# Identity products ahead of three of TensorE's waits in the attention and linear-attention units of a two-layer decoder step

## The reference

```
layer 0:  h = rmsnorm(x);  p = h @ w_in_even      (q, k, v of 4 heads; q, k, v, decay, gate of 4 linear heads)
          attention, prompt:  o = (softmax(q1 k1' + bias) - lam * softmax(q2 k2' + bias)) @ v      causal
          attention, sample:  the same against 4096 cached rows of k and v per sequence, by a page table
          a_out = rmsnorm(o, g_da)
          linear attention (chunks of 16):  att = tril(qe ke');  o = att v + qe S
                                            S = exp(b_last) * S + kd' v
          o = rmsnorm(o, g_gla) * silu(gate)
          x += rmsnorm([a_out, o] @ w_out_even);  x += rmsnorm(relu(h @ w_up)^2 @ w_down)
layer 1:  a gated recurrence with a width-4 convolution in place of attention, then the same kind of MLP
```

## Time and profile before

| | us |
|---|---|
| median of three runs | 1482.88 |
| the profiled execution's own time | 1480.3 |
| its span, first to last instruction | 1478.5 |
| TensorE busy, of the span | 1355.1 |
| VectorE busy | 1112.2 |
| ScalarE busy | 679.3 |
| Pool busy | 334.6 |

### The profile page before, as it was taken

One profiled execution on the slowest core, in us unless ns is written; L12 is line 12 of the kernel. 1 busy time (PEld: TensorE's weight loads), 2 busy tenths in 40 slices (PEclk: granted clock), 3 DMA queues, 4 the chain that ended last, 5 costly groups with the idle time before them and its releaser, 6 DMA issues.

```text
span 1478.5 us, 26838 instructions
## 1 busy us (share of the span) xinstructions
PE 1355.1 (92%) x10976; PEld 1216.4 (82%) x10976; DVE 1112.2 (75%) x1737; ACT 679.3 (46%) x1225; POOL 334.6 (23%) x268
## 2 busy tenths in 40 slices
PE   5999967878778898999999999899989999999997
PEld 5999933345333598999999999899988999999996
DVE  5799887775886626885968779789557868869695
ACT  4322245533343434544535446478444544445355
POOL 2567677775776200000000000000000000000000
PEclk9999978897776899999999999999999999999999
DMA  8788689999888831142231413222212132412321
GB/s 293 274 298 275 235 330 378 365 382 352 311 328 305 315 115 43 54 135 87 79 122 58 143 58 115 86 86 88 87 58 85 60 122 80 136 65 89 117 81 59
DMA packets 126865, 249.38 MB, mean 169 GB/s; under 512 B 5251, under 2 KB 107415, under 8 KB 110096
## 3 DMA queue, kind: packets, MB, share of 16 engines
q0 software_dynamic: 18432, 134.23, 24.0%
q1 hardware_dynamic: 105180, 109.46, 22.8%
q10 hardware_dynamic: 3132, 3.98, 0.9%
HBM read 239.99 MB, written 7.73 MB: 168 GB/s over the span
## 4 chain that ended last, share of the span: by engine, by line
PE 53%; issue 26%; DVE 9%; POOL 4%; ACT 4%; DMA 3%; POOLq 0%; ACTq 0%; SPq 0%; DVEq 0%
PE PS L2105 32%; PE PS L2183 10%; POOL PROD L764 3%; PE PS L2330 2%; DVE SC L1488 2%; DMA KV<-in_cache_v,CIDX 2%; PE PS L2491 1%; POOL KV L836 1%; PE PS L2414 1%; DVE ST L1726 1%; DMA XIN<-in_x_prompt 1%; ACT W_hi L894 1%; DVE W_lo L1421 1%; PE PS L2229 1%; PE PS L2317 1%
## 5 line engine op out<-in xcount | busy, mean ns | idle before, releaser
L2105 PE MATMUL PS<-H_hi,W_hi 128*128 128x260 f32 x1936 | 402.8, 288 | 20.8 <-DVE H_lo L1463 9.7
L2105 PE MATMUL PS<-H_hi,W_lo 128*128 128x260 f32 x1936 | 397.4, 286 | 0.0
L2105 PE MATMUL PS<-H_lo,W_hi 128*128 128x260 f32 x1936 | 396.9, 286 | 0.0
L2105 PEld LDWEIGHTS PS<-H_hi,W_hi 128*128 128x128 f32 x1936 | 305.5, 192 | 26.3 <-issue 22.6
L2105 PEld LDWEIGHTS PS<-H_hi,W_lo 128*128 128x128 f32 x1936 | 304.6, 192 | 0.0
L2105 PEld LDWEIGHTS PS<-H_lo,W_hi 128*128 128x128 f32 x1936 | 304.0, 191 | 0.0
L2183 PE MATMUL PS<-U_hi,G_hi 128*128 128x260 f32 x896 | 255.0, 285 | 0.3 <-DVE U_lo L1854 0.3
L2183 PE MATMUL PS<-U_hi,G_lo 128*128 128x260 f32 x896 | 253.5, 283 | 0.0
L2183 PE MATMUL PS<-U_lo,G_hi 128*128 128x260 f32 x896 | 252.1, 281 | 0.0
L1421 DVE TENSOR_TENSOR W_lo<-RAW,W_hi 128x2048 fp32r<-128x2048 f32 x58 | 132.9, 2291 | 99.9 <-ACT W_hi L894 99.8
L764 POOL TENSOR_TENSOR PROD<-KV,QB 128x1024 f32<-128x1024 f32 x64 | 153.9, 2405 | 98.6 <-DVE SC L1488 91.2
(11 more groups left out here) (329 smaller groups left out, 1939.9 us busy)
## 6 DMA issues: line engine op xcount, KB each, us to landing
RAW<-in_w_up SPq DMA_DIRECT2D x32, 1024.0 KB, 5.4
RAW<-in_w_down SPq DMA_DIRECT2D x32, 1024.0 KB, 4.9
RAW<-in_w_in_even SPq DMA_DIRECT2D x13, 1024.0 KB, 6.6
RAW<-in_w_in_odd SPq DMA_DIRECT2D x8, 1024.0 KB, 5.3
RAW<-in_w_out_even SPq DMA_DIRECT2D x4, 1024.0 KB, 8.5
RAW<-in_w_out_odd SPq DMA_DIRECT2D x4, 1024.0 KB, 4.8
x_saved<-X ACTq DMA_DIRECT2D x1, 2080.0 KB, 13.5
X<-x_saved SPq DMA_DIRECT2D x1, 2080.0 KB, 8.9
```

Source lines behind the costliest of these rows:

```text
L2105: t = MM_(PS[:, 2 * bank + j, 0:HALF], w[:, ch.wslot, k, cols], x[:, k, halves[j]], start=k == 0 and n == 0, stop=k == KT - 1 and n == 2)
```

## The change

A helper `keep_clock(count)` is added, and called at three places. It issues `count` products of the identity with itself into bank 3 of the PSUM, columns 0 to 127. Nobody reads these results: the next writer of the place starts its sum afresh. The products wait for nothing and signal nothing.

```diff
+        def keep_clock(count):
+
+            for _ in range(count):
+                MM_(PS[:, 3, 0:P], IDENT, IDENT, start=True, stop=True)
...
             if u >= 2:
                 normalise(u - 2)
                 pe.wait_ge(nev_done, u - 1)
+            keep_clock(3)
             pe.wait_ge(at_copied, u + 1)
...
         for u, (tb, hp) in enumerate(GLA_UNITS):
             if u:
+                keep_clock(4)
                 inner_products(u)
...
             pe.wait_ge(st_ready, 8 * u + 8)
             if u:
                 normalise(15 + u)
+            keep_clock(4)
             if u:
                 pe.wait_ge(nev_done, outputs_done(16 + u))
```

## The result

The change made the kernel slower. Eight runs of each gave a median of 1488.22 us (1482.86 to 1495.51) against 1481.61 us (1478.13 to 1484.05), a ratio of 1.0058 with a 95% interval of 1.0039 to 1.0077. The forecast was 4 us faster. Two things show at once: the sign is the other one, and the times of the changed kernel spread over 13 us where those of before spread over 6.

The account below looks back on a forecast made before the run. TensorE mostly bounds the kernel, with loads, VectorE and Pool also binding in the attention and linear units. Adding 17.0 us and getting 21.1 back nets -4.1: median 1482.9 becomes 1478.8 us, 8-in-10 range 1466 to 1492.

Parts of the forecast that it names:

- What a product costs: On TensorE, one further identity product in a group takes 0.22 us at the full clock, 0.425 at the low one.
- The cost on the path: Products delay the attention units by 7.4 us and the linear units by 9.6, together 17.0 us.
- the 60%: Attention units: share of the 48 products' 12.3 us taken as on the path, giving 7.4 us.
- cover: Linear units: 7 us of the products' 16.6 us hidden inside existing TensorE waits.
- What the clock gives back: Less low clock returns 6.2 us in the attention units, 11.9 in the linear units, 3.0 more: 21.1 us.
- the weaker term: Three long low-clock stretches, not counted as avoided, each end sooner: some 4.6 us in all, 3 taken.
- At twice the clock half of a busy time goes: In seven low-clock stretches of both unit stages, half of TensorE's 41.9 us busy time was the basis for the gain.
- My own first rival: No change that shows: VectorE and Pool set the pace in both stages, median at 1484 us; chance 0.29.
- The rule that everything behind 507 us merely shifts: From 507 us on the change touches nothing; the stretch from the output projection on stays at 971 us.
- The slower one: Clock falls behind waits for loads and Pool, attention products stay uncovered: +12 us, median 1495; chance 0.27.
- The break-even: 17 us must come back, meaning some 40 of the 118 us at the low clock must go.
- the first of my own signs: Prediction is wrong if the linear units' clock rises and their stage keeps its length, forecast at 147 to 151 us.

Follow-up runs that it names:

- e9: The changed kernel with each identity product reading one column instead of 128: 1.0079 of the kernel before.
- e5: The kernel before, unchanged, run and traced again: 1.0000 of the kernel before.
- e6: The changed kernel, run again without further edits: 1.0029 of the kernel before.
- e18: The changed kernel, run again beside e17: 1.0015 of the kernel before.
- e2: The changed kernel with only the linear units' 60 products, those of the attention units taken out: 0.9981 of the kernel before.
- e12: The changed kernel with six products instead of three in the attention units, four kept in the linear ones: 1.0054 of the kernel before.
- e16: Against the changed kernel, 48 attention products moved inside the copy wait, 32 linear ones kept in theirs, none ahead of the transposes: 1.0008 of before.
- e17: The changed kernel with the attention products moved inside the wait for the normalised output's copy, all 60 linear products kept: 0.9987 of the kernel before.
- e1: The changed kernel with only the attention units' 48 products, both calls of the linear units taken out: 1.0014 of the kernel before.
- e13: The changed kernel with 18 further products in the waits between the linear units and the output projection: 1.0059 of the kernel before.
- e15: The changed kernel, unedited, a further trace of one execution: 1482.89 us.
- e14: The changed kernel, unedited, a further trace of one execution: 1495.97 us.

## Why the prediction was wrong

The stages of the traces, in us. "None" are traces without products in that stage; for the last two rows it is the kernel before alone.

| | none | one column (e9) | changed kernel, 5 traces | attention products in the wait |
|---|---|---|---|---|
| attention units | 136.4, 137.9, 138.8, 135.1, 141.8: mean 138.0 | 143.8 | 138.0, 139.6, 143.2, 139.2, 138.7: mean 139.7 | 131.8, 133.2, 139.2, 132.2, 132.2: mean 133.7 |
| linear units | 115.7, 119.7, 117.4, 117.9: mean 117.7 | 122.5 | 112.0, 116.0, 122.6, 112.9, 116.1: mean 115.9 | |
| between them | 16.6, 16.3 | 17.2 | 17.9, 17.5, 17.8, 17.4, 18.2: mean 17.8 | |
| from the output projection on | 971.1, 970.8 | 971.3 | 973.4, 972.3, 970.4, 972.7, 974.7: mean 972.7 | |

**What a product costs** was right. In the kernel after a group of three took 0.94 us at the full clock and a group of four 1.16 us, so a further one costs 0.22, as forecast.

**The cost on the path** was put at 7.4 us for the attention units and 9.6 for the linear ones. With e9 as the kernel that pays and gets nothing, it is 143.8 - 138.0 = 5.8 us and 122.5 - 117.7 = 4.8 us, with 0.8 us between the stages: 11.4 us of 17.0. By its ratio e9 pays 0.79%, 11.7 us. This is one trace, and it holds more low clock than the kernel before, so it is an estimate. By it the 60% for the attention units was good, and the linear units had more cover than I counted.

**What the clock gives back** is the step that failed, by the size of its term. The prediction had 21.1 us. The fall of the low clock itself was forecast well: from the first product with v to the output projection it was 116 us before (133 in e5) and 78, 72, 102, 68 and 66 us in the five traces after, where I had 68, or less with the weaker term. But the time that came back is 143.8 - 139.7 = 4.1 us in the attention units (forecast 6.2) and 122.5 - 115.9 = 6.6 us in the linear ones (forecast 14.9 with the weaker term), 10.7 in all. "At twice the clock half of a busy time goes" holds for TensorE; that it "all lies on the path" doesn't. In the linear units low clock fell by some 38 us from e9 to the mean of the changed kernel, and TensorE's busy time by 15 us, from 108 to 93. Only 6.6 us of these reached the stage. The rest became idle time of TensorE, 14 us in e9 and 21 to 26 in the five traces, in waits for loads, masked copies and the clamp. My own first rival had named the reason with the earlier trace rows, a unit at 0.91 as long as one at 0.68, and I gave it its own chance but took no discount for it in the sum. It was half right: much of the gain was lost there, and less of the cost.

The runs give a second measure of this term, without e9. Over the executions of the kernel before, 17 to 35 in each of five comparisons, the time rose by 0.20 to 0.32 us for each us more at the low clock (worked out from the span and mean clock of each execution). A long execution may have a low clock because of its waits, so this is not a proof of the direction. In e6 and e18 the low clock was 47 and 51 us less than in before beside them; by the 0.25 and 0.22 of these chips that gives 11.7 and 11.2 us back, by the half it would be over 20. With the measured losses of 4.3 and 2.2 us the cost is then 16 and 13 us. So the cost lies between 11 and 16 us, not far under the 17.0 of the sum, and what came back near 11 us, half of the 21.1.

**A term that wasn't in the sum** is the start of the output projection. I had that stretch unchanged at 971 us. In four of five traces after it begins at the low clock and lasts 972.3 to 974.7 us; the mean of the five is 1.8 us over before. In e2, e12, e16 and e17 it begins at the low clock too and lasts 972.2 to 974.0 us. The rule that everything behind 507 us merely shifts fails where the clock carries over.

(Two kernels with the same attention code are left out of the table: e1 with 135.9 us and e13 with 142.2; with them the mean is 139.5.) The terms then add up: attention +1.7, between +1.3, linear -1.8, output projection +1.8 (and the stretch ahead of it even, 22.1 us against 21.9), together +3.0 us on the mean of five traces; the three comparisons gave 1.0058, 1.0029 and 1.0015, which is 8.6, 4.3 and 2.2 us. What stays open is why the first came out at the high end. On one chip the changed kernel took 1482.9 us with 68 us of low clock from the first product with v to the output projection (e15) and 1496.0 with 102 us (e14). How many executions of the second kind eight runs hold is chance in part.

**The rivals.** The slower one, +12 with fewer than 30 us of low clock gone, had the right sign and place, not the right cause: the low clock fell by 38 us on the mean in the two stages. The rule of the Trainium skill that spoke against the change (TensorE: Matmul & The Clock Gate, section "HAM oscillation — how this bites in real kernels") would have left the low clock where it was. The traces disagree with that reading: products in gaps of around 1 us took it from 99 us in the two stages to between 49 and 87 us. The Trainium skill's section "A second HAM failure mode: psum-queue depth-cycling" on the same page, which names idling in small pieces, agrees with them. The break-even was too low by the same error. From e9 to the changed kernel the low clock of the two stages fell from 113 to 61 us on the mean, for 10.7 us: a fifth, as in the executions above. At that rate 11.4 us of cost ask for 55 us less, more than half of what there is.

**The signs named for the profile after.** Clock from the last attention product to the output projection, the cut of the earlier trace rows, 0.84 and 0.85 in the first two traces against 0.86 forecast, of the attention units 0.89 and 0.91 against 0.91: right, but 0.80 and 0.86 in e14. The wait ahead of the linear outputs gone: right. VectorE's wait for the scores up by 5 us: 1.2 in the first trace, 12.5 in e14. Linear stage at 147 to 151 us for 153.4: no; in the same cut it took 154.3. By the first of my own signs, a higher clock of the linear units in a stage that keeps its length, the prediction was wrong.

## What to carry to other kernels

Put a filler that is to hold TensorE's clock inside a wait: in front of the semaphore that TensorE really waits for by the trace, not of one that is always satisfied when it gets there. In three pairs on the same chips the filler inside the wait was 4.3 to 7.7 us faster. Whether it is worth having at all is not shown here: of the five kernels with covered attention products two lie below 1 with their intervals, three don't. Count the clock's gain at what the neighbours let through: here 0.2 to 0.3 of the low clock's time came back, not the half. Price such a filler with one-column products, which take nearly the time and gain no clock, before adding it.

## What the runs showed of the hardware

- An identity product of one column takes nearly as long as one of 128: median record 250 ns against 275, and a group of three 0.83 us against 0.94 at the full clock. The mean clock was 0.929 with 108 of them, 0.936 without, and 0.952 with 108 of 128 columns on another chip, where it was 0.936 without as well.
- The low clock can carry over into a stretch that is bound by TensorE: the output projection and all behind it took 972.2 to 974.7 us in the eight traces in which it began at the low clock, and 970.4 to 972.3 us in the other twelve.
- The time depends on the chip: the kernel before had medians of 1481.6 to 1491.8 us in these comparisons, and the changed kernel's executions spread by up to 18 us within one of them.
